# Keeping the activations of the first block with features on partitions: no transposes, modulation summed by columns on VectorE

## What is computed

```python
def modulate(h, shift, scale):
    return h * (1 + scale[:, None, :]) + shift[:, None, :]

def swiglu(h, w_gate, w_up, w_down):
    return (jax.nn.silu(h @ w_gate) * (h @ w_up)) @ w_down
...
    c_act = jax.nn.silu(c)

    for l in range(DEPTH):
        mod = c_act @ ada_w[l] + ada_b[l]
        (sh1, sc1, g1, sh2, sc2, g2, sh3, sc3, g3) = jnp.split(mod, 3 * N_SUBLAYERS, axis=-1)

        h = modulate(rms_norm(x, ffn1_norm[l]), sh1, sc1)
        x = x + 0.5 * g1[:, None, :] * swiglu(h, ffn1_w_gate[l], ffn1_w_up[l], ffn1_w_down[l])
```

## Time and profile before

| what | value |
| --- | --- |
| median of three executions | 1358.2 us |
| the profiled execution | 1359.12 us |
| its span | 1357.3 us |
| mean granted TensorE clock | 0.971 |
| busy share of TensorE, VectorE, ScalarE | 94%, 77%, 45% |
| bytes read from HBM | 294 MB, 218 GB/s over the span |
| share of the chain that ended last | TensorE 83%, VectorE 11%, ScalarE 3% |

### The profile page before, as it was taken

One profiled execution on the slowest core, in us unless ns is written; L12 is line 12 of the kernel. 1 busy time (PEld: TensorE's weight loads), 2 busy tenths in 40 slices (PEclk: granted clock), 3 DMA queues, 4 the chain that ended last, 5 costly groups with the idle time before them and its releaser, 6 DMA issues.

```text
span 1357.3 us, 21395 instructions
## 1 busy us (share of the span) xinstructions
PE 1282.4 (94%) x8744; PEld 1167.1 (86%) x8744; DVE 1050.6 (77%) x1380; ACT 608.8 (45%) x868; POOL 136.3 (10%) x156
## 2 busy tenths in 40 slices
PE   1999999999999999999999999999978889899998
PEld 1899998988999998999999889999976667799997
DVE  7789897777878648898877868999469996755554
ACT  4533334566333336443445664333362235634443
POOL 0010000000005100000000000000007770000000
PEclk8899999999999998999999989999989989999999
DMA  9699997442886653999974427444542204355551
GB/s 374 250 365 347 354 360 287 143 153 90 299 311 261 260 189 140 351 342 357 364 290 153 156 69 290 186 186 185 197 144 78 78 16 139 121 201 197 197 196 48
DMA packets 55774, 296.12 MB, mean 218 GB/s; under 512 B 6560, under 2 KB 6816, under 8 KB 32416
## 3 DMA queue, kind: packets, MB, share of 16 engines
q1 hardware_dynamic: 46496, 228.21, 46.0%
q0 software_dynamic: 9216, 67.11, 12.6%
HBM read 294.25 MB, written 1.05 MB: 218 GB/s over the span
## 4 chain that ended last, share of the span: by engine, by line
PE 83%; DVE 11%; ACT 3%; issue 1%; DMA 1%; SPq 0%; DVEq 0%; ACTq 0%
PE gu_bank L541 17%; PE gu_bank L542 16%; PE gu_bank L543 16%; PE y_bank L543 8%; PE y_bank L542 8%; PE y_bank L541 8%; DVE ysc L1766 2%; DVE dn_lo L1369 1%; PE t_bank L541 1%; PE t_bank L543 1%; PE t_bank L542 1%; DVE acc_m L1315 1%; DVE xn L1432 1%; DVE vin L1761 1%; DMA pro<-ada 1%
## 5 line engine op out<-in xcount | busy, mean ns | idle before, releaser
L541 PE MATMUL gu_bank<-hT_hi,gu_hi 128*128 128x256 f32 x1760 | 494.6, 281 | 8.3 <-DVE hT_lo L1356 8.0
L543 PE MATMUL gu_bank<-hT_hi,gu_lo 128*128 128x256 f32 x1760 | 491.2, 279 | 0.0
L542 PE MATMUL gu_bank<-hT_lo,gu_hi 128*128 128x256 f32 x1760 | 491.1, 279 | 0.0
L541 PEld LDWEIGHTS gu_bank<-hT_hi,gu_hi 128*128 128x128 f32 x1760 | 334.2, 190 | 15.7 <-issue 9.6
L542 PEld LDWEIGHTS gu_bank<-hT_lo,gu_hi 128*128 128x128 f32 x1760 | 334.8, 190 | 5.4 <-issue 1.0
L543 PEld LDWEIGHTS gu_bank<-hT_hi,gu_lo 128*128 128x128 f32 x1760 | 333.7, 190 | 0.0
L1374 DVE TENSOR_TENSOR gu_lo<-raw_gu,gu_hi 128x2048 fp32r<-128x2048 f32 x105 | 241.0, 2295 | 40.5 <-ACT gu_hi L1037 40.5
L1049 ACT ACTIVATE sg<-gu_bank 128x256 f32<-128x256 f32 x110 | 42.3, 385 | 450.0 <-PE gu_bank L543 449.9
L1037 ACT ACTIVATE gu_hi<-raw_gu 128x2048 fp32r<-128x2048 f32 x105 | 201.1, 1915 | 11.9 <-DMA raw_gu<-ffn_gu 11.7
L542 PE MATMUL y_bank<-dn_lo,act_hi 128*128 128x512 f32 x440 | 174.3, 396 | 0.0
L543 PE MATMUL y_bank<-dn_hi,act_lo 128*128 128x512 f32 x440 | 174.2, 396 | 0.0
(11 more groups left out here) (337 smaller groups left out, 1803.6 us busy)
## 6 DMA issues: line engine op xcount, KB each, us to landing
raw_gu<-ffn_gu SPq DMA_DIRECT2D x110, 1024.0 KB, 6.0
stage<-ada POOLq DMA_DIRECT2D x64, 1024.0 KB, 7.8
raw_dn<-ffn_dn SPq DMA_DIRECT2D x110, 512.0 KB, 3.8
ring<-mix_w SPq DMA_DIRECT2D x72, 512.0 KB, 3.7
pro<-ada SPq DMA_DIRECT2D x5, 1024.0 KB, 12.3
gate_b<-gate_rows SPq DMA_DIRECT2D x6, 512.0 KB, 3.8
stage<-ada SPq DMA_DIRECT2D x2, 1024.0 KB, 20.8
x<-x_in SPq DMA_DIRECT2D x1, 1024.0 KB, 6.3
```

The costliest lines, as they stand in the source:

```text
L541: pe.matmul(to, a[0], b[0], start=start, stop=False)
L542: pe.matmul(to, a[0], b[1], start=False, stop=False)
L543: return pe.matmul(to, a[1], b[0], start=False, stop=stop)
```

## The change

In the first block, x is kept with features on partitions (8 chunks of 128 × 256). The transposes go, and what varies by feature becomes a per-partition scalar.

- The weights of the modulation come transposed, one column tile of 128 features × 1024 at a time (0.5 MB), 144 in all, through eight slots. `column(q)` multiplies a tile by c, which stands on all partitions as a row (`c_row`), and its accumulator output is the finished column of scale, shift or gate. 16 columns are summed ahead of the first product, 48 in the first feed-forward part of each layer, 24 and 8 in the second ones. The ones-products of `modulation` and `gate` go.
- A norm: ScalarE squares each chunk, VectorE adds four of them up in three instructions (`partial`), TensorE sums over partitions with five ones-products of 128 × 256 (`sums`), ScalarE takes the root, VectorE the reciprocal of 128 × 256 (`root`); then chunk by chunk `scaled`, the hi part with the shift on ScalarE, and `shifted_lo`.
- The first products of a sublayer go chunk by chunk of the features (`by_chunk`), for three column tiles of a mixer at a time, or for blocks 0 and 1 of a feed-forward part (`pair`; the very first takes block 0 alone).
- Down products and the mixer's output products have the weights stationary and the activations moving: 24 products of 256 columns in place of 12 of 512. Banks that several chunks share are first cleared by a product of zeros (`clear`, 128 × 512).
- The residual is eight instructions straight from PSUM.
- At a mixer's end, the first block of the next feed-forward part is split whole (`split_block0`), and the second one's two halves as well, all ahead of the residual.
- The final norm and the second block's first are taken together, with two sums; 16 transposes bring x back to tokens there.
- Fillers of 64 bytes shift `dn_hi`, `act_hi` and the mixer's latents. TensorE's loops are written out.

```diff
 MOD_ORDER = (("m", 0), ("g", 0), ("m", 1), ("m", 2), ("g", 1), ("g", 2), ("m", 3), ("g", 3), ("m", 4), ("m", 5), ("g", 4), ("g", 5))
-MOD_CHUNKS = {"m": 8, "g": 4}
-CHUNKS = 72
+MOD_COLS = {"m": 16, "g": 8}
+COLS = 144
+STAGES = 8
+PRO = 16
...
-        x = sb(ctx, "x", [P, TT, D])
+        x = sb(ctx, "x", [P, KC, S])
...
+        sq_x = xn[:, :, :].rearrange("p t d -> p (t d)").rearrange("p (c s) -> p c s", c=KC)
+        x_tok = x[:, :, :].rearrange("p c s -> p (c s)").rearrange("p (t d) -> p t d", t=TT)
...
+        zero = sb(ctx, "zero", [P, 16], F32R)
         dn_hi = sb(ctx, "dn_hi", [P, SLOTS, D], F32R)
         dn_lo = sb(ctx, "dn_lo", [P, SLOTS, D], F32R)
+        sb(ctx, "dn_end", [P, 16])
...
+        stage = sb(area, "stage", [P, STAGES, D])
...
+        def unit_home(m):
+
+            if m < 2:
+                return [a[:, 1, 1 - m, :, :].rearrange("p c n -> p (c n)") for a in (gu_hi, gu_lo)]
+            slot = (m + 2) % SLOTS
+            return dn_hi[:, slot, :], dn_lo[:, slot, :]
...
+        def y_part(dc, mixer):
+
+            if mixer or dc < 4:
+                return yb[dc // 2][:, S * (dc % 2):S * (dc % 2 + 1)]
+            return (*yb[2:], *tb)[dc - 4][:, 0:S]
...
+            for q in range(STAGES):
+                columns_of(q)
+            sp_.dma_start(x[:, :, :], x_in.rearrange("(c p) s -> p c s", p=P)).then_inc(x_loaded, 16)
+            for q in range(STAGES, STAGES + 4):
+                columns_of(q)
+            load_gu(0, 0)
+            for q in range(STAGES + 4, PRO):
+                columns_of(q)
+            load_gu(1, 1)
+            for g in range(2):
+                load_dn(g, g)
...
             def fetch(q):
 
-                pool.wait_ge(acc_step, summed(q - 2))
-                pool.dma_start(stage[:, q % 2, :], ada[q]).then_inc(ada_loaded[q % 2], 16)
-
-            for q in range(PRO, 44):
+                pool.wait_ge(mod_step, q - STAGES + 1)
+                pool.dma_start(stage[:, q % STAGES, :], ada[q]).then_inc(ada_loaded[q % STAGES], 16)
...
-                for j in range(16):
-                    last = pe.matmul(tb[0][:, j:j + 1], acc_m[:, M_SLOT[m], tok(j)], ones[:, 0:1], start=True, stop=True)
-                last.then_inc(mod_ps, 1)
...
+            def sums(kt):
+
+                to = ss_bank(kt)
+                if kt and kt % 3 != 2:
+                    pe.wait_ge(prod_done, FB * (2 * (kt // 3) + (kt % 3 > 0)) - 1)
+                pe.wait_ge(part_done, kt + 1)
+                for c in (0, 4, 5, 6, 7):
+                    if c:
+                        pe.wait_ge(sq_done, KC * kt + c + 1)
+                    last = pe.matmul(to, ones[:, :], sq_x[:, c, :], start=c == 0, stop=c == KC - 1)
+                last.then_inc(ss_ps, 1)
...
+            def clear(bank_):
+
+                pe.matmul(bank_[:, :], zero[:, 0:1].to_broadcast([P, P]), zero[:, 0:1].to_broadcast([P, 512]), start=True, stop=False)
...
-            def gate(l, m):
-
-                pe.wait_ge(acc_step, summed_at("g", 3 * l + m))
-                for b in range(2):
-                    pe.matmul(tb[b][:, :], ones[:, :], acc_g[:, half(b)], start=True, stop=True).then_inc(gate_ps, 1)
...
+            def by_chunk(kt, targets):
+
+                for c in range(KC):
+                    pe.wait_ge(hT_hi_done, KC * kt + c + 1)
+                    if c < KC - 1:
+                        for to, w, first, _, _ in targets:
+                            hi, lo = w(c)
+                            pe.matmul(to, hi, hT_hi[:, c, :], start=first and c == 0, stop=False)
+                            pe.matmul(to, lo, hT_hi[:, c, :], start=False, stop=False)
+                        pe.wait_ge(hT_lo_done, KC * kt + c + 1)
+                        for to, w, _, _, _ in targets:
+                            pe.matmul(to, w(c)[0], hT_lo[:, c, :], start=False, stop=False)
+                    else:
+                        pe.wait_ge(hT_lo_done, KC * kt + c + 1)
+                        for to, w, _, final, signal in targets:
+                            last = passes(to, w(c), (hT_hi[:, c, :], hT_lo[:, c, :]), False, final)
+                            if signal is not None:
+                                last.then_inc(signal, 1)
...
+                kt = 3 * (f // 2) + 2 * (f % 2)
+                gate_up_first(kt, range(2 if pair else 1))
+                if not pair:
+                    gate_up(1)
+                for bank_ in yb[:2]:
+                    clear(bank_)
+                down(0)
+                if pair:
+                    down(1)
+                    gate_up(2)
+                for n in range(2 if pair else 1, FB - 3):
+                    gate_up(n + 1)
+                    down(n)
+                gate_up(FB - 2)
+                gate_up(FB - 1)
+                down(FB - 3)
...
+                for dc in range(3):
+                    down_part(FB - 2, dc)
                 hidden_ready(FB - 1)
-                for h in range(2):
-                    down_part(1, 0, h, final=True).then_inc(y_ps, 1)
-                down_part(0, 1, 1).then_inc(dn_used, 1)
-                for h in range(2):
-                    down_part(1, 1, h, final=True).then_inc(y_ps, 1)
+                for dc in range(KC):
+                    if dc >= 3:
+                        last = down_part(FB - 2, dc)
+                        if dc == KC - 1:
+                            last.then_inc(dn_used, 1)
+                    down_part(FB - 1, dc, dc % 2 == 1 or dc >= 4).then_inc(y_ps, 1)
...
+                tiles = [(tile_bank()[:, 0:S], split_unit(l, n)) for n in range(3)]
+                by_chunk(3 * l + 1, [(to, lambda c, w=w: [a[:, tok(c)] for a in w], True, True, tile_ps) for to, w in tiles])
...
+                for bank_ in yb:
+                    clear(bank_)
...
+            sums(0)
+            pe.wait_ge(rms_ready, 1)
+            clear(gu_bank[0])
             for l in range(DEPTH):
-                for m in range(3):
-                    k = 3 * l + m
-                    if k == 0:
-                        transposes(k)
-                        modulation(k, l, m)
-                    else:
-                        modulation(k, l, m)
-                        transposes(k)
-                    if m == 1:
-
-                        pe.wait_ge(mod_done, k + 1)
-                        gate(l, m)
-                        mixer(l)
-                    else:
-                        ffn(2 * l + m // 2, k, lambda: gate(l, m))
+                ffn(2 * l, l > 0)
+                sums(3 * l + 1)
+                mixer(l)
+                sums(3 * l + 2)
+                for bank_ in gu_bank:
+                    clear(bank_)
+                ffn(2 * l + 1, True)
+                sums(3 * l + 3)
+                if l < DEPTH - 1:
+                    pe.wait_ge(prod_done, FB * (2 * l + 2))
+                    pe.wait_ge(rms_ready, 3 * l + 4)
+                    for bank_ in gu_bank:
+                        clear(bank_)
+            sums_weighted()
 
 
...
+            def squares(kt):
+
+                for c in range(KC):
+                    if kt:
+                        act.wait_ge(x_ready, KC * (kt - 1) + c + 1)
+                    else:
+                        act.wait_ge(x_loaded, 16)
+                    act.activation(sq_x[:, c, :], x[:, c, :], ACT.Square).then_inc(sq_done, 1)
...
+                for c in range(KC):
+                    act.wait_ge(t_ready, KC * kt + c + 1)
+                    act.activation(hT_hi[:, c, :], hT[:, c, :], ACT.Identity, bias=mods[:, KC + c:KC + c + 1]).then_inc(hT_hi_done, 1)
...
+            def column(q):
...
+                    dve.wait_ge(ada_loaded[q % STAGES], 16 * ((q - PRO) // STAGES + 1))
+                to = at + (MOD_COLS["m"] if kind == "g" else 0)
+                summing.did(dve.scalar_tensor_tensor(mod_slot(q), mod_slot(q), 1.0, c_row[:, :], ALU.mult, ALU.mult, accum_out=mod_raw[:, k, to:to + 1]))
+
+            def gains(l, m):
+
+                k, at = 3 * l + m, L_ADA + 3 * KC * m
                 dve.wait_ge(lc_loaded, 16 * l + 16)
-                dve.wait_ge(mod_ps, k + 1)
-                step.then(dve.tensor_tensor(mods[:, :], tb[0][:, 0:16], lc[:, L_ADA + 16 * m:L_ADA + 16 * m + 16], ALU.add))
-                dve.scalar_tensor_tensor(gs[:, :], mods[:, KC:2 * KC], 1.0, lc[:, L_NORM + KC * m:L_NORM + KC * m + KC], ALU.add, ALU.mult)\
-                   .then_inc(mod_done, 1)
-                dve.wait_ge(mod_done, k + 1)
...
+            def shifts(l, m):
+                k, at = 3 * l + m, L_ADA + 3 * KC * m + KC
+                dve.wait_ge(mod_step, summed_at("m", k))
+                dve.tensor_tensor(mods[:, KC:2 * KC], mod_raw[:, k, KC:2 * KC], lc[:, at:at + KC], ALU.add).then_inc(mod_done, 1)
+
+            def gate(l, m):
+
+                k, at = 3 * l + m, L_ADA + 3 * KC * m + 2 * KC
+                dve.wait_ge(mod_step, summed_at("g", k))
```

(62 more changed lines are left out.)

769 lines of the change are left out of this document (408 added, 361 removed).

## The result

The changed kernel takes 1365.96 us (median of 5 runs, 1363.67 to 1366.55), the kernel before 1358.2: a ratio of 1.0052, 95% interval 1.0036 to 1.0069. It is slower by half a per cent; 1346.5 us was forecast. Its profiled execution has a span of 1364.0 us, 6.7 more than before.

The account below looks back on a forecast made before the run. TensorE's back-to-back products, plus its waits for norms, were taken as the bound. The terms summed to −11.7 us, from 1359.1 us profiled to 1347.4, or 1346.5 us as a median; range 1332 to 1364 us.

Parts of the forecast that it names:

- Gates: Feed-forward parts where a gate is made: its products leave TensorE, 1.9 us four times, −7.6 us.
- down products: Feed-forward blocks: 24 products of 256 columns replace 12 of 512, −0.07 us a block, −6.2 us over 88 blocks.
- mixers' rates: Mixers: z tiles at 113.5 instead of 120 ns a product, about −1.1 us a mixer, −2.2 us.
- prologue: Start of the kernel: TensorE starts at 47.4 us, first down product at 60.7, +5.0 us.
- the column: VectorE's SCALAR_TENSOR_TENSOR 128×1024 with accumulator output: 1.3 us each, 48 in the first part, covered at 164 of 180 us.
- Rival A: VectorE, first feed-forward parts: column takes double, 2.35 us; about 1456 us. Chance 0.10 for 1.45 and above, 0.05 for double.
- D: Rival, first feed-forward parts: the wide DMA queue binds, +9 us in each, 1365 us; chance 0.05.
- Norm behind a mixer: Mixer's last product to first down product, twice: residual waits behind splits on VectorE, TensorE restarts after 8.8 us; +3.5 us.
- Norms ahead of a mixer and between the layers: Sublayer boundaries: TensorE restarts after 5.7 us; −1.9 us each ahead of mixers (twice), −1.3 us between the layers (once).
- The state-space loop: Second block's VectorE-bound loop: loses one lo split of 1.2 us, so −1.2 us.
- The last part: Last feed-forward part: keeps its token order, 0 us.
- Rival C: Boundaries and prologue: split hidden behind the mixer's last products, prologue packs closer, restarts after 5 us; about 1335 us; chance 0.15.

Follow-up runs that it names:

- second profiles: The changed kernel and the kernel before, each unchanged and profiled a second time: 1365.98 and 1357.14 us.
- the zeros: Changed kernel plus products of zeros in TensorE's idle stretches at the five boundaries inside the first block: 1354.07 us, ratio 0.9958 to the kernel before.

## Why the prediction was wrong

The sign was wrong, and the range missed the time by 2 us. The sum was off by 18.5 us, which lie in the places where engines wait for each other and in the last part; by its own steps:

- **Gates, down products, mixers' rates, prologue, the column**: right. A part of 172.1 us takes 168.7 now, −3.4 us, against −3.45 forecast; that the table comes so near for all four has some luck in it, since the first profile of the kernel before had a slow stretch of 1.9 us and the changed one slow blocks of 1.2 us. Rival A needed 1.45 us for a column, it takes 1.30. The Trainium skill's rule beside it ("Vector Engine (DVE) Microarchitecture Reference", section "7. Points that are easy to get wrong": this instruction with two fp32 sources in SBUF "halves throughput", as nothing is left for the accumulator) does not show here: 1220 ns with the accumulator, 1283 for the same shape without. The clock of the first part is 1.00 and its blocks take 8.16 us at a DMA share of 0.91: D falls. The 64-byte fillers are a premise of these terms, as the kernel without them showed.
- **Norm behind a mixer (+1.75 each; measured +3.8 and +4.5, in the second profiles +5.8 and +5.7)**: this is the step that failed: "square, ones-product, root, reciprocal and the first chunk take 4.4 more". They took 6.3 (from 323.42 to 329.73). The mechanism was named, VectorE's queue ahead of the residual, and its effect on the residual's start was right to 0.6 us (318.83 for 318.2). Of the 1.9 us, about 1 is the clock: I reckoned that the last ones-product follows the last square at once. It does at full clock; behind 3.56 us of idle time the five take 3.48 us instead of 2.43, since the clock falls to half while they run. The other 0.9 are terms that were too small even at full clock: with the halves behind the residual the same chain takes 5.3 us (321.17 to 326.43). From the restart to the first down product it was 14.2 us for 13.4. The working had a slip too: 323.1 and 4.4 give a restart at 327.5, not 327, and 8.8 + 10.9 + 2.5 are 22.2, not the 22.8 that the sum used.
- **Norms ahead of a mixer and between the layers**: restart after 6.5 us instead of 5.7 (the terms as I listed them give only 5.35). The half clock behind it costs what the execution makes of it: 2.7 to 2.8 us in the first profile, 1.4 to 1.8 in the second, as the zeros measured, where 1.4 and 1.6 were forecast. I had also counted the fast rate of the first three column tiles twice (0.5 us each). And between the layers I left out the first activation behind the last chunk: products end at 533.36, the first down product starts at 534.62. That the second profiles have −1.4 us there, nearly the forecast, is luck of the clock.
- **The state-space loop (−1.2; measured +1.75, in the second profiles +0.75)**: I counted one lo part fewer and did not ask whose hi part VectorE would wait for when each is taken a step earlier. It is the wait of 3.06 us, and it costs 1.7. With the two a step later the loop takes 142.7 to 142.9 us without zeros; whether the 1.2 us was there to be had can't be told, since the kernel before took 142.8 to 144.2.
- **The last part (0; measured +4.75)**: 4.0 of it is the spacing of 117.8 ns, for which no step of mine allowed, since neither instructions nor order change there. I knew of two spacings of the same product and treated them as tied to places. Its cause is open.

Rival C (1335 us) said that the splits could hide behind the mixer's last products. They can, but only by another order than the one the change has.

## What to carry over

A boundary is priced by its idle stretches, not only by its chain: here waits of TensorE of 2.2 to 3.6 us cost up to 4 us more a boundary, at half clock, in what followed, whoever caused them, and in some executions nothing. Read the granted clock behind every restart, take more than one profile before a stretch is given a price, and fill the wait with products that nobody needs, or shorten it. When work is taken a step earlier on one engine, look up where its input stands in the queue of the engine that makes it.

## What the hardware showed that I had not expected

- The same 256-wide product runs back to back at 113.4, 117.8 or 120 ns. The offsets of its operands have a part in it: with fillers of 64 bytes the first block's parts run at 113.3 ns in nearly all blocks; without them every second block has 117.9, and the mixer's output products 120. Elsewhere the slower spacing differs from one execution to the next (a feed-forward part of 172.1 or 174.0 us in one kernel), or is bound to the program with an unknown cause (the last part).
- The same idle stretch between two layers was followed by a granted clock of 0.50 for some us in one execution and by 1.00 throughout in another: 21.9 and 19.1 us.
- Products of zeros hold the granted clock at 1.00 as real ones do.
- An accumulator output on VectorE costs a read of 83 ns, and the instruction itself 1220 ns, less than the 1283 of the sum it replaced.
